# Linear-attention scan of a two-layer block: order of gates and low parts changed, layer 0's scan joined to its projection

## The chip, the core and the metric

The kernel runs on one core of a Trainium2 chip. The metric is device time in microseconds for one execution. All matrix products are done on TensorE as three products of split operands: each float32 matrix is held as a high part (rounded to the engine's fast fp32r form) and a low part (what the rounding left out), and high x high, high x low and low x high are summed.

## The reference, cut to what matters

Two blocks follow each other over 1024 tokens of width 1024. The change touches only the first, which has two layers. A layer normalises its input, projects it, and runs a linear-attention branch and a differential-attention branch beside each other:

```
h = rms_norm(x, g) * (1 + scale) + shift;  proj = h @ w_in
gq, gk, gv = silu(causal_depthwise_conv(concat(gq, gk, gv), conv_w))       # 8 tiles of 128 channels
log_a = log_sigmoid(glr @ w_gk + b_gk) / 16,  b = cumsum(log_a) in chunks of 64 tokens
k_dec = k * exp(b_end - b);  u = k_dec^T v;  state = exp(b_end) * state + u;  o = q state
o = rms_norm(o) * silu(z)
x = x + gate * (concat(o_gla, o_diff) @ w_out)
```

`shift`, `scale` and `gate` come from one vector: `mod = silu(c) @ w_ada + b_ada`. Those of the next layer are computed in the course of this one.

## The kernel before

The kernel is a row of stages. Within a stage each engine (SyncE for the DMAs, GpSimd, ScalarE, VectorE, TensorE) has a list of instructions in fixed order, and semaphores tie the lists together. Most stages are a block of their own, and a block ends with a barrier of all engines.

**Projection of the linear-attention branch** (`stage_gla_project`, L991, over the helper `stage_project`, L676). Jobs: four with 256 weight columns each, which give eight convolution tiles of two halves; one for `glr`; and the first half of the z weights, which is only loaded and split (`hold`), for use by the scan. For every tile TensorE makes two PSUM halves, ScalarE copies them to `u` (L866) and applies the first tap (L877), VectorE applies three more taps (L900), ScalarE applies SiLU (L883). In layer 0 VectorE also sums the modulation of layer 1: 16 parts of 512 KB are loaded into two buffers (`load`, L951; part k waits until part k-2 is summed) and accumulated with four instructions each (L961, L965). Two parts follow each convolution tile: parts 2n and 2n+1 behind tile n. At the very end VectorE makes the low part of the z weights (L788). ScalarE takes `glr` out of PSUM (L1010) behind the last SiLU.

**The scan** (`stage_gla`, L1072). It runs the recurrence over eight tiles of 128 tokens and, between its small products, 32 units of twelve 512-column matmuls (L1175) that project z and v. Each pair of units fills one PSUM bank (tiles 0 to 3 and 4 to 7 share four banks). Four units are done ahead (`LEAD`), then eleven steps n, each with three units, in TensorE's order: outputs of tile n-2 (L1240), transposes of tile n (L1193, L1195), a unit, decays of tile n-1 (L1211, L1213), gate product of tile n (L1202), a unit, states of tile n-1 (L1226), transposes of the result of tile n-3 (L1251), a unit. The decays write the bank from which `ktok` and `vtok` of the following tile are read, so they wait for both.

ScalarE's order in a step: squares of tile n-2 (L1324), `vtok` of tile n (L1300), root (L1332), decays (L1307), the gate's three functions (L1315 to L1319), `empty_y` (L1340). SiLU of the z units (`gates`, L1346) needs another function table than the rest and loads it, and the old one again: four tiles at the end of step 1 and four at the end of step 3. The high parts of the scan's four weight tiles (L1063) stand before the steps and at the ends of steps 2, 3 and 7. GpSimd makes the low parts (L1068) as soon as the high ones are there.

VectorE's order in a step: `ktok` (L1386), the normed result (L1427), `kdec` (L1394), the log gate (L1401), the state update (L1415), the copies of the summed gate (L1441), four accumulations of this layer's gate vector (L965), copies of v units (L1435). In layer 0 the last thing TensorE does is `columns` (L975): 32 products of one column that turn the sums for the next layer into columns, from which VectorE makes `shift` and `gain`.

**After the scan** the next block projects the differential branch (L824 again). In layer 1 the projection is preceded in its block by the output stage of layer 0, so its scan has always begun a new block.

Of the kernel before, what the change touches and what calls it, by code (L numbers as in the profile page):

```python
# [15 lines left out]
F32 = mybir.dt.float32  # L16
# [903 lines left out]
class Modulation:  # L920
# [52 lines left out]
    def columns(self, pe, bank, c0):  # L973
        for c in range(2 * KC):
# [16 lines left out]
def stage_gla_project(nc, m, jobs, feat, glrT, mod, b_gate, base, block, opening):  # L991
# [3 lines left out]
    nconv = 8  # L995

# [37 lines left out]
    def sp_job(sp, q, t):  # L1034
        if t == 0:
            mod.load_bias(sp, q, b_gate)
        for n in range(mod.early):
            if t == (0 if n < 2 else (n + 6) // 4):
# [6 lines left out]
                  sp_job=sp_job, begun=0 if opening else KC - 2, base=base, block=block, opening=opening)  # L1045


class ScanWeights:
# [7 lines left out]
    def __init__(self, nc, ctx, m, stage, jobs, slots):  # L1056
        self.nc, self.m, self.jobs, self.slots = nc, m, jobs, slots
        self.s_raw, self.s_hi, self.s_lo = semaphores(nc, ctx, m, stage, "wraw whi wlo")
        self.raw = ctx.enter_context(m.tensor(stage + "_wraw", [P, KC // 2 * 512], F32))
# [10 lines left out]


def stage_gla(nc, m, feat, glrT, zv, w_gk, b_gk, jobs, mod, slot):  # L1072
# [9 lines left out]
    with ExitStack() as ctx:  # L1082
        (s_w, s_turn, s_kv, s_gate, s_abs, s_act, s_la, s_suf, s_dec, s_kd, s_u, s_st, s_o, s_sq, s_r,
         s_y, s_yt, s_mix, s_dve, s_unit, s_slot, s_zev, s_vev, s_mraw0, s_mraw1, s_macc, s_spread, s_gated,
         s_own, s_wzero) = semaphores(
            nc, ctx, m, "gla", "w turn kv gate abs act la suf dec kd u st o sq r y yt mix dve unit slot zev vev mraw0 "
            "mraw1 macc spread gated own wzero")

        def sb(name, shape):
            return ctx.enter_context(m.tensor("gla_" + name, shape, F32))  # L1090

        wgk = sb("wgk", [RANKS + 1, GLA_QK])
        ktok, vtok = sb("ktok", [P, 2, GLA_QK]), sb("vtok", [P, 2, GLA_W])
        la, dec = sb("la", [P, 2, GLA_QK]), sb("dec", [P, 2, GLA_QK])
        gexp = sb("gexp", [P, GLA_QK])
        aend = sb("aend", [P, 2, 4])
        kdec = sb("kdec", [P, 2, GLA_QK])
        state = sb("state", [P, 4, pairs, GLA_DV])
        sq, ssq, r = sb("sq", [P, GLA_H, GLA_DV]), sb("ssq", [P, 2, GLA_H]), sb("r", [P, 2, GLA_H])
        y = sb("y", [P, 2, GLA_W])  # L1100
        weights = ScanWeights(nc, ctx, m, "gla", jobs, [1 - slot, 1 - slot, slot, slot])
        ps = m.ps
        block = ctx.enter_context(nc.Block())


        U, KG, TB = (4, 7), 5, 6
        STEPS = range(NT + 3)
        LEAD, UNITS, BANKS = 4, 4 * NT, 4
        n0 = mod.early
        late = len(mod.parts) - n0  # L1110

        def part_of(n):
            return n

        def o_of(h):
            return ps[:, U[h % 2], P * (h // 2):P * (h // 2) + P]

        def unit(u):


            job, w = u // 16, u % 16
            block4 = w // 4
            second = block4 in (1, 2)
            tile = w % 4 + 4 * (block4 // 2)
            return job, tile, second, block4 % 2 == 0

        def slot_of(job, second):
            return slot if job == second else 1 - slot

        @block.sync  # L1130
        def _(sp):
            load_tile(sp, weights.raw, weights.jobs[0], weights.s_raw)
            sp.wait_ge(s_wzero, 1)
            sp.dma_start(wgk[0:RANK, :], w_gk).then_inc(s_w, 16)
            sp.dma_start(wgk[RANK_LO:RANKS, :], w_gk).then_inc(s_w, 16)
            sp.dma_start(wgk[RANKS:RANKS + 1, :], b_gk).then_inc(s_w, 16)
            for k in range(2):
                mod.load(sp, (s_mraw0, s_mraw1), s_macc, n0 + k, n0)
            for k in range(2, late):
                if k in (part_of(3), part_of(5), part_of(7)):  # L1140
                    w = 1 + (part_of(3), part_of(5), part_of(7)).index(k)
                    sp.wait_ge(weights.s_lo, w)
                    load_tile(sp, weights.raw, weights.jobs[w], weights.s_raw)
                mod.load(sp, (s_mraw0, s_mraw1), s_macc, n0 + k, n0)
            m.clear_stale(sp)

        @block.gpsimd
        def _(pool):
            pool.memset(wgk[:, :], 0.0).then_inc(s_wzero, 1)
            weights.low(pool)  # L1150

        @block.tensor
        def _(pe):
            def project(u):
                job, tile, second, opens = unit(u)
                if u == 4:
                    pe.wait_ge(weights.s_lo, 1)
                if u == 16:
                    pe.wait_ge(weights.s_lo, 2)
                if u == 20:  # L1160
                    pe.wait_ge(weights.s_lo, 3)
                if opens and job == 0 and tile >= BANKS:
                    pe.wait_ge(s_zev, tile - BANKS + 1)
                if opens and job == 1 and tile < BANKS:
                    pe.wait_ge(s_zev, BANKS + tile + 1)
                if opens and job == 1 and tile >= BANKS:
                    pe.wait_ge(s_vev, tile - BANKS + 1)
                out, toks = ps[:, tile % BANKS, :], slice(P * tile, P * tile + P)
                hi, lo = (t[:, slot_of(job, second), :].rearrange("p (c n) -> p c n", c=KC // 2)
                          for t in (m.w_hi, m.w_lo))  # L1170
                for c in range(KC // 2):
                    lc = KC // 2 * second + c
                    a_hi, a_lo = m.hT_hi[:, lc, toks], m.hT_lo[:, lc, toks]
                    for k, (l, r) in enumerate(((a_hi, hi[:, c, :]), (a_hi, lo[:, c, :]), (a_lo, hi[:, c, :]))):
                        mm = nc.tensor.matmul(out, l, r, start=(opens and c == 0 and k == 0),  # L1175
                                              stop=(not opens and c == KC // 2 - 1 and k == 2))
                if not opens:
                    mm.then_inc(s_unit, 1)
                elif u in (11, 27):
                    mm.then_inc(s_slot, 1)  # L1180

            def turn(i):

                toks = slice(P * i, P * i + P)
                if i >= 1:
                    pe.wait_ge(s_kv, 2 * i)
                    pe.wait_ge(s_la, i)
# [3405 lines left out]
```

## Time and profile before

| | |
|---|---|
| median of 3 runs | 2449.79 us (2449.46 to 2450.44) |
| the profiled execution | 2450.71 us, its span 2449.0 us |
| TensorE busy | 2338.1 us, 95% of the span |
| VectorE, ScalarE, GpSimd busy | 1259.6 us, 1056.0 us, 632.8 us |
| TensorE clock granted, mean | 0.982 |
| layer 0: first product of the scan to first of the next stage | 156.65 to 297.79 us |
| layer 1: the same | 748.43 to 884.62 us |

Times inside the span are counted from its start. The busy time of TensorE counts a matmul at either clock alike, so the granted clock of a stretch has to be read beside it: 1.00 is 2.4 GHz, 0.50 is 1.2 GHz, and values between are mixtures of the two.

### The profile page before, as it was taken

The page shows a single profiled execution, that of the slowest core. Times are in us where ns is not written, and L with a number is a line of the kernel's source. Part 1 is how long each engine was busy: PE and PEld are TensorE (multiplying, and loading weights), DVE is VectorE, ACT ScalarE, POOL GpSimd, SP SyncE. Part 2 cuts the span into 40 slices and gives each one's busy share as a digit, 9 for nine tenths or more (in the row PEclk, how much of TensorE's full clock was granted, in tenths as well). Part 3 has the DMA queues.
Part 4 walks back from the last instruction along what each step waited for, and adds up shares of the span by engine and source line. Part 5 has one row for each costly group of instructions (what it writes and reads, how often), then busy time and mean ns, then how long its engine had stood idle before and what let it go on. Part 6 is the DMA issues. An engine that isn't in the chain of part 4 may idle for free. (4 is left out here: it accounts for less than half of the span.)

```text
span 2449.0 us, 33123 instructions
## 1 busy us (share of the span) xinstructions
PE 2338.1 (95%) x12824; PEld 1905.5 (78%) x12824; DVE 1259.6 (51%) x1768; ACT 1056.0 (43%) x2254; POOL 632.8 (26%) x419
## 2 busy tenths in 40 slices
PE   6998999889999999988999999998999999999999
PEld 4776787777887777777888887677888888888887
DVE  5854403785552520586553166561586777774121
ACT  4435313674543432376342546563653333334221
POOL 2201021133310122033232112112224444466130
PEclk8999999899999999999999999999999999999999
DMA  7432010103212211002211100003222222237231
GB/s 248 129 130 70 27 52 18 35 1 123 101 43 70 70 52 35 18 19 85 96 60 46 57 1 5 18 14 129 78 78 78 91 82 86 78 132 251 82 138 43
DMA packets 139073, 181.87 MB, mean 74 GB/s; under 512 B 8700, under 2 KB 102307, under 8 KB 138917
## 3 DMA queue, kind: packets, MB, share of 16 engines
q1 hardware_dynamic: 137877, 179.74, 21.4%
q8 instruction: 103, 1.69, 0.3%
q14 instruction: 53, 0.43, 0.1%
q10 hardware_dynamic: 1040, 0.00, 0.0%
HBM read 151.41 MB, written 28.31 MB: 73 GB/s over the span
## 5 line engine op out<-in xcount | busy, mean ns | idle before, releaser
L824 PE MATMUL ps<-w_hi,hT_hi 128*128 128x512 f32 (+1 forms) x384 | 142.8, 372 | 1.8 <-PEq L1082 1.8
L824 PE MATMUL ps<-hT_hi,w_hi 128*128 128x512 f32 x360 | 141.2, 392 | 2.8 <-PEq L274 2.8
L824 PE MATMUL ps<-w_hi,hT_lo 128*128 128x512 f32 (+1 forms) x384 | 142.8, 372 | 0.0
L824 PE MATMUL ps<-w_lo,hT_hi 128*128 128x512 f32 (+1 forms) x384 | 142.8, 372 | 0.0
L3978 POOL TENSOR_TENSOR w_lo<-ffn_sums,w_hi 128x512 fp32r<-128x512 f32 x76 | 96.7, 1294 | 171.9 <-ACT w_hi L4160 171.9
L824 PE MATMUL ps<-hT_lo,w_hi 128*128 128x512 f32 x360 | 140.6, 390 | 0.0
L824 PE MATMUL ps<-hT_hi,w_lo 128*128 128x512 f32 x328 | 128.3, 391 | 0.0
L1175 PE MATMUL ps<-w_hi,hT_hi 128*128 128x512 f32 x256 | 110.0, 430 | 12.9 <-ACT vd L1346 6.6
L4028 PE MATMUL ps<-ffn_t_hi,w_hi 128*128 128x512 f32 x304 | 118.4, 389 | 0.7 <-DVE ffn_u L4337 0.7
L4028 PE MATMUL ps<-ffn_t_hi,w_lo 128*128 128x512 f32 x304 | 118.3, 389 | 0.0
L4028 PE MATMUL ps<-ffn_t_lo,w_hi 128*128 128x512 f32 x304 | 118.3, 389 | 0.0
L2105 PE MATMUL ps<-w_hi,hT_hi 128*128 128x512 f32 x288 | 113.4, 394 | 4.3 <-PEq L4528 3.0
L2105 PE MATMUL ps<-w_hi,hT_lo 128*128 128x512 f32 x288 | 112.7, 391 | 0.0
L2105 PE MATMUL ps<-w_lo,hT_hi 128*128 128x512 f32 x288 | 112.5, 391 | 0.0
L4337 DVE TENSOR_TENSOR ffn_u<-ffn_u,ps 128x512 f32<-128x512 f32 x95 | 65.1, 685 | 80.4 <-PE ps L4028 77.4
L1175 PE MATMUL ps<-w_lo,hT_hi 128*128 128x512 f32 x256 | 103.9, 406 | 0.0
L1175 PE MATMUL ps<-w_hi,hT_lo 128*128 128x512 f32 x256 | 103.7, 405 | 0.0
L1828 ACT ACTIVATE big<-ps,att_nb 128x640 f32<-128x640 f32 (+7 forms) x128 | 94.2, 746 | 16.2 <-DVE att_nb L1815 15.6
L900 DVE SCALAR_TENSOR_TENSOR glap_cv<-glap_u,cols,glap_cv 128x1024 f32<-128x1024 f32 x48 | 74.6, 1555 | 46.6 <-ACT glap_cv L877 45.5
L1510 DVE TENSOR_REDUCE qk_ssq<-difp_sq 128x8 f32<-128x512 f32 x16 | 11.0, 686 | 168.6 <-ACT difp_sq L1498 168.6
L1815 DVE TENSOR_REDUCE att_nb<-ps 128x1 f32<-128x640 f32 (+7 forms) x88 | 86.5, 1022 | 18.7 <-PE ps L1805 18.5
L1068 POOL TENSOR_TENSOR w_lo<-gla_wraw,w_hi 128x2048 fp32r<-128x2048 f32 x8 | 37.1, 4636 | 212.3 <-ACT w_hi L1063 212.3
(564 smaller groups left out, 6534.5 us busy)
## 6 DMA issues: line engine op xcount, KB each, us to landing
ffn_raw<-in_ffn_w_up SPq DMA_DIRECT2D x40, 512.0 KB, 4.6
mix_gla<-in_w_ada SPq DMA_DIRECT2D x32, 512.0 KB, 3.4
ffn_raw<-in_ffn_w_down SPq DMA_DIRECT2D x30, 512.0 KB, 4.4
xres<-big SPq DMA_DIRECT2D x24, 512.0 KB, 2.6
hid<-ffn_f SPq DMA_DIRECT2D x22, 512.0 KB, 2.6
ffn_sums<-hid SPq DMA_DIRECT2D x44, 256.0 KB, 3.6
difp_raw<-in_w_in SPq DMA_DIRECT2D x10, 1024.0 KB, 5.0
open_ada<-in_w_ada SPq DMA_DIRECT2D x8, 1024.0 KB, 9.8
```

Of the source, the lines that this page charges most:

```text
L824: mm = nc.tensor.matmul(out, l, r, start=(job.part != 1 and c == 0 and k == 0), stop=(job.evac and c == job.chunks - 1 and k == len(pairs) ...
L900: ins = nc.vector.scalar_tensor_tensor(out=cv, in0=u[:, j:j + S], scalar=self.tap_col(n, j), in1=cv, op0=ALU.mult, op1=ALU.add)
L1068: pool.tensor_tensor(self.m.w_lo[:, self.slots[k], :], self.raw[:, :], self.m.w_hi[:, self.slots[k], :].bitcast(F32), ALU.subtract).then_i ...
L1175: mm = nc.tensor.matmul(out, l, r, start=(opens and c == 0 and k == 0), stop=(not opens and c == KC // 2 - 1 and k == 2))
L1510: nc.vector.tensor_reduce(ssq[:, i, 0:G], groups(q.sq[:, i % 2, :]), AX_X, ALU.add).then_inc(q.extra["sum"], 1)
L1815: self.nc.vector.tensor_reduce(self.nb[:, n % 4, mp, 0:nh], self.s_of(n, mp), AX_X, ALU.max, negate=True).then_inc(self.s_neg, 1)
L1828: ins = self.nc.scalar.activation(self.p_of(n, mp)[:, k, :], self.s_of(n, mp)[:, k, :], ACT.Exp, bias=self.nb[:, b, mp, k:k + 1], accum_ou ...
L2105: mm = nc.tensor.matmul(out, l, r, start=(first and c == 0 and n == 0), stop=(last and c == KC // 2 - 1 and n == 2))
L3978: pool.tensor_tensor(lo, op.source(n), hi.bitcast(F32), ALU.subtract).then_inc(s_lo, 1)
L4028: mm = nc.tensor.matmul(ps[:, bank(s, acc), :], l[:, c, :], r_[:, c, :], start=(first and c == 0 and i == 0), stop=(c == 3 and i == 2), sk ...
L4337: nc.vector.tensor_tensor(dst, left, ps[:, bank(s, k), :], ALU.add).then_inc(signal, 1)
```

## The change

- The scan's body is no longer a block of its own: it takes a context, a block and `q`, the projection's buffers and semaphores. In layer 0 it runs in the projection's block, without a barrier between. There it uses the projection's `raw` for its weights and the convolution buffers for `state`, `sq` and `y`, and waits on the projection's semaphores. In layer 1 it keeps its own block.
- In layer 0 the first unit does its eight products with high weights first, and waits for the low weights only then. Before the first unit TensorE waits for all 16 modulation parts, before every leading unit for its bank.
- The modulation parts follow the convolution tiles otherwise: parts 0 to 9 as before, 10 to 12 behind tile 5, 13 to 15 behind tile 6, none behind tile 7.
- `columns` is split in four and stands behind the four leading units; the gains follow on VectorE before step 0.
- The low parts of the scan's weights are made by VectorE, in both layers: before the steps and at the ends of steps 2, 4 and 8.
- ScalarE does `vtok` before the squares; the SiLUs come two at the end of step 0, two at the end of step 1, four at the end of step 3; the third high part moves from step 3 to step 4.

The core of the diff, leaving out the scan's re-indentation:

```diff
+    def part_tile(k):
+        return k // 2 if k < 10 else 5 + (k - 10) // 3
...
-            for k in (2 * n, 2 * n + 1):
-                if k < mod.early:
+            for k in range(mod.early):
+                if part_tile(k) == n:
                     mod.accumulate(dve, s_mraw(q), q.extra["macc"], k, 0)
...
+    def low_one(self, dve, k):
+        dve.wait_ge(self.s_hi, k + 1)
+        self.nc.vector.tensor_tensor(self.m.w_lo[:, self.slots[k], :], self.raw[:, :],
+                                     self.m.w_hi[:, self.slots[k], :].bitcast(F32), ALU.subtract).then_inc(self.s_lo, 1)
...
+    if q:
+        state = q.cv[:, 0, :].rearrange("p (n h d) -> p n h d", n=4, h=pairs)
+        sq = q.cv[:, 1, 0:GLA_W].rearrange("p (h d) -> p h d", h=GLA_H)
+        y = q.u[:, 0, 0:2 * GLA_W].rearrange("p (b n) -> p b n", b=2)
...
+    LOW_AT = (2, 4, NT)
...
+        if q:
+            sp.wait_ge(q.s_lo, q.made)
         load_tile(sp, weights.raw, weights.jobs[0], weights.s_raw)
...
+        if q:
+            sp.wait_ge(q.extra["macc"], mod.HALF * mod.early)
...
-            weights.low(pool)
...
+            if u == 0 and q:
+                order = [(c, k) for ks in ((0, 2), (1,)) for c in range(KC // 2) for k in ks]
+            for c, k in order:
+                lc = KC // 2 * second + c
+                if u == 0 and q and (c, k) == (0, 1):
+                    pe.wait_ge(q.s_lo, q.made)
...
+            if i == 0 and q:
+                for b in (*U, KG, TB):
+                    pe.wait_ge(q.free[b], 2)
+                pe.wait_ge(q.extra["silu"], 8)
...
+        if q:
+            pe.wait_ge(q.s_hi, q.made)
+            pe.wait_ge(q.free[U[0]], 2)
+            pe.wait_ge(q.extra["macc"], mod.HALF * mod.early)
         for u in range(LEAD):
+            if q:
+                pe.wait_ge(q.free[u], (q.units - u + NBANK - 1) // NBANK)
             project(u)
+            if mod.ahead:
+                mod.columns(pe, U[0], 0, range(u * 2 * KC // LEAD, (u + 1) * 2 * KC // LEAD)).then_inc(s_cols, 1)
...
-                elif n == NT + 2 and mod.ahead:
-                    pe.wait_ge(s_gated, 2)
-                    mod.columns(pe, KG, 0).then_inc(s_spread, 1)
...
         for n in STEPS:
-            if 0 <= n - 2 < NT:
-                squares(n - 2)
             if n < NT:
                 values(n)
             if 0 <= n - 2 < NT:
+                squares(n - 2)
                 root(n - 2)
...
-            if n == 1:
-                gates(range(4))
+            if n == 0:
+                gates((0, 1))
+            if n == 1:
+                gates((2, 3))
             if n == 2:
                 act.wait_ge(s_slot, 1)
                 weights.high(act, 1)
             if n == 3:
-                gates(range(4, 8))
-                weights.high(act, 2)
+                gates((4, 5, 6, 7))
+            if n == 4:
+                weights.high(act, 2)
...
+        weights.low_one(dve, 0)
+        if mod.ahead:
+            dve.wait_ge(s_cols, LEAD)
+            mod.gains(dve, Count(dve, s_own), m.layer + 1, U[0], 0)
...
+            if n in LOW_AT:
+                weights.low_one(dve, 1 + LOW_AT.index(n))
...
+                if not block:
+                    retire(m)
                 stage_gla_project(nc, m, glas[l], m.big, glrT, mod,
-                                  a["b_ada"][l, 2 * D:3 * D].rearrange("(c p) -> c p", c=1), base, block, opening)
+                                  a["b_ada"][l, 2 * D:3 * D].rearrange("(c p) -> c p", c=1), base, block, opening,
+                                  None if block else scan)
                 if block:
                     block.__exit__(None, None, None)
-                retire(m)
+                    retire(m)
+                    with ExitStack() as c3:
+                        scan(c3, c3.enter_context(nc.Block()), None)
```

## Rows read from the trace of the kernel before

**Rows 1.** The page's engine table: busy us, share of the span, instructions.

```profile
PE 2338.1 (95%) x12824; PEld 1905.5 (78%) x12824; DVE 1259.6 (51%) x1768; ACT 1056.0 (43%) x2254; POOL 632.8 (26%) x419
```

**Rows 2.** Waits of TensorE, 140 to 300 us: total us, times, longest.

```profile
PE ps L1175 <- PEq L682: 5.2, 1, 5.2
PE ps L1175 <- ACT vd L1346: 3.3, 1, 3.3
PE ps L1211 <- ACT gla_vtok L1300: 2.0, 1, 2.0
PE ps L1211 <- DVE gla_ktok L1386: 0.9, 1, 0.9
```

**Rows 3.** TensorE by stretches: window, length, busy (instructions), granted clock, DMA share, GB/s.

```profile
151.47:169.99 18.52, 13.34 (x49) 0.82 0.35 115
187.96:192.50 4.54, 4.54 (x13) 0.62 0.00 0
214.88:217.83 2.95, 2.95 (x14) 1.00 1.06 398
247.26:259.73 12.47, 12.47 (x90) 1.00 0.13 43
748.43:759.43 11.00, 11.00 (x48) 1.00 0.59 195
777.59:782.96 5.37, 5.37 (x13) 0.51 0.00 0
297.79:301.45 3.66, 3.66 (x9) 0.55 0.69 213
```

**Rows 4.** ScalarE's timeline, layer 0: start, duration, operation [idle before <- releaser].

```profile
151.15 1.05 ACT L1010 ACTIVATE glrT<-ps 48x512 f32<-48x512 f32 x2
...
180.57 0.60 ACT L1300 ACTIVATE gla_vtok<-ps 128x512 f32<-128x512 f32 x1 [5.06 <-PE ps L1195]
...
187.31 2.06 ACT L1346 ACTIVATE vd<-ps 128x512 f32<-128x512 f32 x4
189.39 1.28 ACT L1347 ACT_TABLE_LOAD   x1
...
224.51 1.91 ACT L1063 ACTIVATE w_hi<-gla_wraw 128x2048 fp32r<-128x2048 f32 x1
```

**Rows 5.** VectorE's accumulations and GpSimd's low part, layer 0, same columns.

```profile
194.50 2.04 DVE L965 SCALAR_TENSOR_TENSOR gate<-mix_gla,cact,gate 128x256 f32<-128x256 f32 x4
...
206.56 6.27 DVE L965 SCALAR_TENSOR_TENSOR gate<-mix_gla,cact,gate 128x256 f32<-128x256 f32 x4
...
206.68 4.83 POOL L1068 TENSOR_TENSOR w_lo<-gla_wraw,w_hi 128x2048 fp32r<-128x2048 f32 x1 [38.28 <-ACT w_hi L1063]
```

**Rows 6.** VectorE at the end of layer 0's projection, same columns.

```profile
146.22 3.93 DVE L900 SCALAR_TENSOR_TENSOR glap_cv<-glap_u,cols,glap_cv 128x1024 f32<-128x1024 f32 x3 [2.98 <-ACT glap_cv L877]
...
154.04 2.28 DVE L788 TENSOR_TENSOR w_lo<-glap_raw,w_hi 128x2048 fp32r<-128x2048 f32 x1
```

**Rows 7.** TensorE at the scan's end and the next stage's start, both layers.

```profile
292.49 0.63 PE L1251 MATMUL ps<-ident,gla_y 128*128 128x128 f32 x4
293.26 3.73 PE L975 MATMUL ps<-ones,mix_gla 128*128 128x1 f32 x32
297.79 0.47 PE L824 MATMUL ps<-w_hi,hT_hi 128*128 128x512 f32 x1 [0.80 <-PEq L1082]
...
882.96 0.63 PE L1251 MATMUL ps<-ident,gla_y 128*128 128x128 f32 x4
884.62 0.47 PE L824 MATMUL ps<-w_hi,hT_hi 128*128 128x512 f32 x1 [1.03 <-PEq L1082]
```

**Rows 8.** Loads of modulation parts 12 and 15: issue, then us to landing.

```profile
131.74 0.37 SPq L951 DMA_DIRECT2D mix_gla<-in_w_ada  x1
mix_gla<-in_w_ada SPq DMA_DIRECT2D x1, 512.0 KB, 4.4
...
mix_gla<-in_w_ada SPq DMA_DIRECT2D x1, 512.0 KB, 3.6
```

More of the change, by code:

```diff
@@ L971, in spread_gate, with columns @@
                                      start=True, stop=True)
-    def columns(self, pe, bank, c0):
-        for c in range(2 * KC):
+    def columns(self, pe, bank, c0, chunks):
+        for c in chunks:
             mm = self.nc.tensor.matmul(self.m.ps[:, bank, c0 + c:c0 + c + 1], self.acc[:, P * c:P * c + P],
@@ L988, in gains, with stage_gla_project @@
                                                 in1=cols[:, m.C_NORM:m.C_NORM + KC], op0=ALU.add, op1=ALU.mult))
-def stage_gla_project(nc, m, jobs, feat, glrT, mod, b_gate, base, block, opening):
+def stage_gla_project(nc, m, jobs, feat, glrT, mod, b_gate, base, block, opening, scan):
     conv = ConvTiles(nc, CONV_K, lambda n, j: m.col(m.C_CONV + 8 * j + n), None,
@@ L1044, in stage_gla_project, with __init__ @@
                   setup=lambda ctx, q: conv.setup(ctx, q, "glap"), dve_before=dve_before, dve_after=dve_after,
-                  sp_job=sp_job, begun=0 if opening else KC - 2, base=base, block=block, opening=opening)
+                  sp_job=sp_job, begun=0 if opening else KC - 2, base=base, block=block, opening=opening, tail=scan)
 class ScanWeights:
-    def __init__(self, nc, ctx, m, stage, jobs, slots):
+    def __init__(self, nc, ctx, m, stage, jobs, slots, raw=None):
         self.nc, self.m, self.jobs, self.slots = nc, m, jobs, slots
         self.s_raw, self.s_hi, self.s_lo = semaphores(nc, ctx, m, stage, "wraw whi wlo")
-        self.raw = ctx.enter_context(m.tensor(stage + "_wraw", [P, KC // 2 * 512], F32))
+        self.raw = raw if raw is not None else ctx.enter_context(m.tensor(stage + "_wraw", [P, KC // 2 * 512], F32))
     def high(self, act, k):
@@ L4473, in build_first, with scan @@
                 mod = Modulation(nc, m, mix_gla, a["w_ada"], l)
+                slot = (len(glas[l]) - 1 + base) % 2
+                weights = [gate_half(a["w_in"][l], 1), *halved("v", [wtile(a["w_in"][l], C_DV, DIFF_W)], DIFF_W), diffs[l][0]]
+                def scan(c, block, q):
+                    stage_gla(nc, m, c, block, q, m.big, glrT, v, a["w_gk"][l],
+                              a["b_gk"][l].rearrange("(c p) -> c p", c=1), weights, mod, slot)
+                if not block:
+                    retire(m)
                 stage_gla_project(nc, m, glas[l], m.big, glrT, mod,
-                                  a["b_ada"][l, 2 * D:3 * D].rearrange("(c p) -> c p", c=1), base, block, opening)
+                                  a["b_ada"][l, 2 * D:3 * D].rearrange("(c p) -> c p", c=1), base, block, opening,
+                                  None if block else scan)
                 if block:
                     block.__exit__(None, None, None)
-                retire(m)
-                base = (len(glas[l]) - 1 + base) % 2
-                weights = [gate_half(a["w_in"][l], 1), *halved("v", [wtile(a["w_in"][l], C_DV, DIFF_W)], DIFF_W), diffs[l][0]]
-                stage_gla(nc, m, m.big, glrT, v, a["w_gk"][l], a["b_gk"][l].rearrange("(c p) -> c p", c=1), weights, mod,
-                          base)
+                    retire(m)
+                    with ExitStack() as c3:
+                        scan(c3, c3.enter_context(nc.Block()), None)
+                base = slot
             with keep:
```

654 lines of the change are left out of this document (325 added, 329 removed).

## The prediction

> **What bounds the kernel now.** I read the page's engine table first: TensorE is busy for 95% of the span [rows 1], so only time in which it stands still, or runs at its lower clock, can come back. Then the waits of TensorE in the two scan stages, because they are what the diff touches. In layer 0 they are four [rows 2]: 5.2 us at the block boundary between projection and scan, and inside the scan 3.3 us for ScalarE's `vd` (L1346), 2.0 us for its `vtok` (L1300), 0.9 us for VectorE's `ktok` (L1386). The three inner waits come again in layer 1, with the same lengths to 0.1 us; its boundary wait is 1.2 us.
>
> Third, the granted clock of the stretches [rows 3]. A normal stretch of twelve 512-column matmuls between two small groups takes 2.95 us. After the `vd` wait it takes 4.54 us at a mean clock of 0.62 in layer 0 and 5.37 us at 0.51 in layer 1; after the `vtok` wait 4.54 us again, in both layers (229.64 and 820.11, rows like the first). The 0.9 us wait leaves no such trace. The first 48 products of the scan take 13.34 us in layer 0 (156.65 to 169.99, the remainder of the row's 18.52 after the wait) and 11.00 us in layer 1, after a wait of only 1.2 us: 2.34 us of clock. A step without a stall takes 12.47 us. So each long stall is paid twice, as idle time and then at 1.2 GHz in place of 2.4 GHz.
>
> **The three inner stalls, both layers.**
> *`vd`, step 1.* ScalarE now does four SiLU evictions at the end of step 1: table load 1.28, four copies 2.06, table load 1.28 [rows 4], begun at 186.0, while TensorE has waited for the first freed bank since 187.96 - 3.28 = 184.7. In the changed order two of them come in step 0, where ScalarE is done with the gate at 175.5 (the 5.06 us of idle before 180.57) [rows 4]. 175.5 + 1.28 + 1.03 (half of 2.06) + 1.28 gives 179.1, and the next thing it must do, `vtok` of tile 1, is not ready before 180.6 [rows 4]. The second pair runs from 186.0 to 189.6 and its banks are asked for a step later, with about 3 us to spare once the stall is gone. The stall goes: 3.28 + 1.60 of clock in layer 0, 3.28 + 2.43 in layer 1. The added pair of table loads lies in idle ScalarE time, at nothing; bare it would be 2.6 us a layer.
> *`ktok`, step 3.* At 206.56 VectorE's four accumulations take 6.27 us, where the same four take 2.04 elsewhere, because GpSimd's 4.83 us low part runs beside them [rows 5]; the `ktok` copy behind them came at 213.2, and TensorE had waited 0.9 for it, since 212.3. In the changed kernel VectorE accumulates until 208.6, makes the low part itself (2.28, the price of the same 128x2048 form on VectorE [rows 6]) until 210.9 and copies `ktok` (0.4) by 211.3. So 0.9 us go, with 1.0 to spare. If the low part took what GpSimd takes, 4.8, `ktok` would be 1.5 us late: those are the two ends, and the row of the same form decides for 2.28.
> *`vtok`, step 4.* ScalarE's four SiLUs end with the table load at 224.5; then come a 1.91 us weight copy and, until `vtok` (0.6) can begin at 227.4, 1.0 us of squares [rows 4]. The change puts both behind it: 224.5 + 0.6 = 225.1, while TensorE, which got it at 228.0 after 2.0 of waiting, asks at 226.0. 2.05 of idle and 1.60 of clock go in each layer. Next in line: the weight copy moves to the end of step 4, followed by VectorE's low part. Counted from that step's start, without stalls: last transposes done at 9.6, `big` copy 0.7, weight copy 1.9, low part 2.3: ready at 14.6, and the unit that needs it comes 5.5 into the next step of 12.47, at 18.0; `ktok` of that step stands behind the low part and is done at 15.0, asked for at about 16. In step 8 the last low part stands ahead of `vd` copies for which TensorE no longer waits; I charge nothing, at most 2.3 a layer.
> Sum: layer 0, 3.3 + 0.9 + 2.0 + 1.6 + 1.6 = 9.4; layer 1, with 2.4 for the first 1.6, 10.2 to 10.3. I take no part of it off; the low end, if one of the three waits stays in each layer, is 3.7 less per layer.
>
> **The column sums (layer 0 only).** 32 one-column matmuls of 3.73 us stand at the stage's very end, and the next stage starts 0.80 us after them [rows 7]. Layer 1 has no such sums: there the last transposes start at 882.96 and the next stage at 884.62, so 1.66 us later. In layer 0 they start at 292.49 and the next stage at 297.79, 5.30 later. Taking the sums away is worth 5.30 - 1.66 = 3.6. Besides, layer 0's next stage starts at a clock of 0.55: nine matmuls in 3.66 us [rows 3], where at full clock (48 in 11.00) it would be 16; 7 x 0.23 = 1.6 us more, which layer 1 does not pay. The same 32 products now stand between the leading units: +3.7 us. Bounds for them: nothing, if they fill waiting time, to 7.5 at half clock.
>
> **The join of layer 0.** The 5.2 us wait ends when VectorE, last of all, has made the low part of the z weights: convolution of tile 7 from 146.22 to 150.15, accumulation of two modulation parts until 154.1, low part 2.28 until 156.3, then the barrier [rows 6]. Without the barrier the first unit needs its bank back (after the last convolution: SiLU, about 1.0, and `glrT`, 0.6 [rows 4]), the high part (there) and all modulation parts; the low part comes in only after eight products. Were the convolution still done at 150.15, TensorE would go on at 151.8, almost without a gap.
> But parts 13 to 15 now stand ahead of that convolution. Part 12 is issued at 131.74 and lands 4.4 later, at 136.1 [rows 8]; accumulated until 138.1; convolution 6 (3.93) until 142.0; part 13 (2.02) until 144.1, part 14 until 146.1; part 15 may be issued only at 144.1, because its buffer is that of part 13, and lands 3.6 later at 147.7; accumulated until 149.7; convolution 7 until 153.7; SiLU and `glrT` 1.6: 155.3. If part 12 lands a microsecond earlier, 154.3. I take 155.0: 1.7 us gained of 5.2, ends 1.3 and 4.9. The gap stays at 3.5 us, longer than the 2.05 us after which the clock was seen at its lower level, so the 2.34 us of slow lead stay too. Behind the low part stand SP's load of the next weights, issued at about 156 (before, at the barrier's end, 156.6), the same copy on ScalarE (1.9), and VectorE's 2.28 in place of GpSimd's 4.8: all ready earlier than before, for a unit that comes later than before, at 155.0 + 11.0 + 2.3 + 3.7 = 172. The state memset and the gains (0.5) lie beside the lead, at nothing.
> The Trainium skill ("TensorE: Matmul & The Clock Gate", "Part 1: The HAM clock gate") says that the half-rate clock is the default and that activity releases it. By it, one-column products scattered in a lead that begins slow could keep the lead slow; the trace shows only that after 3.73 us of them in a block the clock is low [rows 3, 7], and that groups of small matmuls between units do not lower it (12.47 us steps at full clock). By the rule at its worst the lead costs 3.7 more for the columns and about 7 for three units; by the row, nothing.
>
> **Sum.** Layer 0: -9.4 - 3.6 - 1.6 + 3.7 - 1.7 = -12.6. Layer 1: -10.3. Together -22.9; I write -23. The stages behind begin with a TensorE-bound projection and a barrier, so all of it arrives at the end. The profiled execution took 2450.71 us (span 2449.0 and 1.7 around it): 2427.7 changed. The median of the three runs is 0.9 below the profiled one: 2426.8.
>
> **Rivals.**
> *A, the join gives everything.* Part 15 is not late, or is accumulated in time: TensorE goes on at 151.8, no slow clock: another 3.2 + 2.3, 2421.3. For it: the layer-1 boundary with 1.2 us shows a full clock. Against: the arithmetic of the two buffers above. 9%.
> *B, ScalarE or VectorE stays the bound in the scan.* The spare times above are 1.0, 0.9 and 1 us. If `vtok` or `ktok` is still late once per layer and the clock falls again (3.7 each): 2434; with the column products at half clock too, 2438. For it: `r` comes 0.6 later because squares now stand behind `vtok`, and all three low parts stand ahead of `ktok` copies. Against: each chain was reckoned from rows with its spare time. 17%. The Trainium skill ("ScalarE: Activation LUTs", "What ACT_TABLE_LOAD costs") gives a drain of about 1.38 us beside each load and advises to finish one table set before switching, which speaks against pairs. By that figure the first pair would end at an estimated 181.9 instead of 179.1 and TensorE, asking at the end of its next unit, some 3 us after the turn at about 180, still would not wait; no run here shows the drain, an activation starts right behind the load.
> *C, the clock of layer 0 stays down.* Starting slow, thinned by one-column products, TensorE could stay at 1.2 GHz through the lead and on into the scan. A unit costs about 2.4 us more at the low clock; from about ten units beyond the usual one on, the gain of 23 is eaten; low through the lead and the first three steps (12 units beyond it, 28.8, and 3.7 for the columns) it is 32.5 us: 2459. Against: from 161.5 on the clock rises in five us of products in a row. 4%.
> *D, the change hardly acts* (the stalls move to another engine at the same size, or clock and waits appear in later stages): within 5 us of before, 2449. 5%.
> My forecast holds 65%, with its own range 2423 to 2431.
>
> **How the numbers follow.** 0.2% is 4.9 us, about what a measurement of this kernel can tell from no change. Faster: forecast, A and B, 91%, less 1 for the tail of B: 0.90. Same 0.05, slower 0.05. The range goes from A's side, 2419, to B's worse end, 2438.
>
> **What would show it.** Waits of TensorE in both scans: L1346, L1300 and `ktok` gone, clock 1.00 from the first turn on; gap between projection and scan in layer 0 near 3.5 us, ended by ScalarE's `glrT`, with convolution 7 ending at about 153.7; layer 0's next stage at full clock; no GpSimd work in the scans. Wrong would be: a wait for `vtok` or `ktok` of over 0.5 us, a low clock after the first unit of step 0, or convolution 7 ending before 151.

## The result, and the profile after

The changed kernel took 2426.95 us in the median of four runs (2421.88 to 2428.38), the kernel before 2450.11 (four runs): the ratio is 0.990, 95% interval 0.988 to 0.992, so faster by 23.2 us. The forecast was 2426.8. The profiled execution took 2426.89 us, its span 2424.8. Layer by layer the forecast was less exact than the total, as will be seen.

The waits of TensorE in both scan stages come first, as [rows 2]: first from 140 to 300 us, then from 700 to 900.

```profile
PE ps L1191 <- ACT glrT L1013: 3.1, 1, 3.1
PE ps L824 <- PEq L682: 1.0, 1, 1.0
...
PE ps L1191 <- PEq L4521: 1.2, 1, 1.2
PE ps L824 <- PEq L4523: 1.0, 1, 1.0
```

The three inner waits are gone in both layers. Of the 5.2 us at the boundary of layer 0, 3.1 are left, now for ScalarE's `glrT`, not for a barrier. The stretches of TensorE that answer to [rows 3] (window, length, busy, granted clock, DMA share, GB/s):

```profile
150.03:169.13 19.10, 15.97 (x80) 0.91 0.34 112
183.80:186.74 2.94, 2.94 (x13) 1.00 0.00 0
227.93:240.40 12.47, 12.47 (x91) 1.00 0.40 127
732.41:743.40 10.99, 10.99 (x48) 1.00 0.58 195
758.00:760.95 2.95, 2.95 (x14) 1.00 0.00 0
283.33:286.99 3.66, 3.66 (x16) 1.00 0.69 223
```

The twelve products in which the `vd` wait was followed by a low clock now take 2.94 and 2.95 us in place of 4.54 and 5.37. The next stage of layer 0 starts with 16 products in 3.66 us, not nine. A step without a stall takes 12.47 us as before. Only the lead of layer 0 is still partly at the low clock.

ScalarE in layer 0, as [rows 4]: the first pair of SiLUs, `vtok` of tile 1 behind it, the four SiLUs of step 3 and `vtok` of tile 4.

```profile
152.44 1.05 ACT L1013 ACTIVATE glrT<-ps 48x512 f32<-48x512 f32 x2
...
176.01 1.09 ACT L1373 ACTIVATE vd<-ps 128x512 f32<-128x512 f32 x2
177.12 1.28 ACT L1374 ACT_TABLE_LOAD   x1
179.76 0.60 ACT L1327 ACTIVATE gla_vtok<-ps 128x512 f32<-128x512 f32 x1 [1.36 <-PE ps L1215]
...
214.19 2.06 ACT L1373 ACTIVATE vd<-ps 128x512 f32<-128x512 f32 x4
216.28 1.28 ACT L1374 ACT_TABLE_LOAD   x1
217.57 0.60 ACT L1327 ACTIVATE gla_vtok<-ps 128x512 f32<-128x512 f32 x1
```

The added table loads end 1.36 us before ScalarE is wanted again. `vtok` of tile 4 is done at 218.2; TensorE asks for it at 218.9, so 0.8 us are spare where the forecast had 0.9. VectorE, first at the end of the projection (as [rows 6]), then around the place of [rows 5]:

```profile
134.50 0.35 DVE L961 TENSOR_SCALAR mix_gla<-mix_gla,cact 128x256 f32<-128x256 f32 x1 [1.98 <-DMA mix_gla<-in_w_ada]
...
136.34 3.92 DVE L900 SCALAR_TENSOR_TENSOR glap_cv<-glap_u,cols,glap_cv 128x1024 f32<-128x1024 f32 x3
...
145.56 2.05 DVE L965 SCALAR_TENSOR_TENSOR mix_gla<-mix_gla,cact 128x256 f32<-128x256 f32 x4 [1.51 <-DMA mix_gla<-in_w_ada]
147.52 3.92 DVE L900 SCALAR_TENSOR_TENSOR glap_cv<-glap_u,cols,glap_cv 128x1024 f32<-128x1024 f32 x3
151.36 2.29 DVE L788 TENSOR_TENSOR w_lo<-glap_raw,w_hi 128x2048 fp32r<-128x2048 f32 x1
...
200.80 2.04 DVE L965 SCALAR_TENSOR_TENSOR gate<-mix_gla,cact,gate 128x256 f32<-128x256 f32 x4
202.76 2.29 DVE L1076 TENSOR_TENSOR w_lo<-glap_raw,w_hi 128x2048 fp32r<-128x2048 f32 x1
204.96 0.42 DVE L1417 COPY gla_ktok<-ps 128x256 f32<-128x256 f32 x1
```

VectorE stands still for part 12 (1.98 us) and for part 15 (1.51 us), and convolution 7 ends at 151.4, after the projection's last product at 150.0. In the scan the accumulations take 2.04 us again, and `ktok` is done at 205.4, 1.1 us before TensorE asks at 206.5.

The end of layer 0's scan, as [rows 7]: the next stage follows the last transposes by 1.66 us in place of 5.30.

```profile
281.67 0.63 PE L1273 MATMUL ps<-ident,glap_u 128*128 128x128 f32 x4
283.33 0.47 PE L824 MATMUL ps<-w_hi,hT_hi 128*128 128x512 f32 x1 [1.03 <-PEq L682]
```

### The profile page after: what moved, and what is told of

It reads as the page before. It is cut to its first block and busy times, and to the rows that moved or that the text cites. A ratio compares the mean times of both kernels' runs of the same rounds, so it can differ in the third digit from the quotient of the medians.

```text
span 2424.8 us, 33122 instructions
## 1 busy us (share of the span) xinstructions
PE 2329.8 (96%) x12824; PEld 1901.2 (78%) x12824; DVE 1266.4 (52%) x1776; ACT 1063.2 (44%) x2258; POOL 596.5 (25%) x411
## 5 line engine op out<-in xcount | busy, mean ns | idle before, releaser
L755 POOL TENSOR_TENSOR w_lo<-difp_raw,w_hi 128x2048 fp32r<-128x2048 f32 x8 | 36.8, 4604 | 391.3 <-ACT w_hi L724 391.3
```

What stands on the lines that cost most here:

```text
L755: pool.tensor_tensor(m.w_lo[:, b, 0:w], raw[:, 0:w], m.w_hi[:, b, 0:w].bitcast(F32), ALU.subtract).then_inc(s_lo, 1)
```

## The experiments

All were timed beside the kernel before on the same chip. In what follows "layer 0" and "layer 1" are the time from the projection's last product to the next stage's first, in one profiled execution: 146.3 and 137.4 us in the kernel before, 133.3 and 126.3 in the changed one. "Lead" is the time from the first leading unit to the first transposes.

**Pairs alone**, on the kernel before.

```diff
-                if n == 1:
-                    gates(range(4))
+                if n == 0:
+                    gates((0, 1))
+                if n == 1:
+                    gates((2, 3))
```

> The kernel before with one edit: the first four SiLU evictions in two pairs, at the ends of steps 0 and 1, in both layers. Theory (the vd wait is a wait for ScalarE's turn, each inner stall stands alone): the 3.3 us wait at L1346 goes in both layers, and the slow stretch behind it (4.54 for 2.95 in layer 0, 5.37 for 2.95 in layer 1): 5.0 + 5.8 = 10.8 us less, about 2439.3; the ktok wait (0.9) and the vtok wait (2.0) stay as they are. Rival (the two extra table loads push vtok): a new wait for vtok of tile 1 of 1 us or more in each layer, the gain at most half: 2444.

Measured: 2434.66 against 2450.64, ratio 0.9938 (0.9926 to 0.9951), 16.0 us less. The waits of layer 0:

```profile
PE ps L1175 <- PEq L682: 5.2, 1, 5.2
PE ps L1211 <- ACT gla_vtok L1300: 2.1, 1, 2.1
PE ps L1211 <- DVE gla_ktok L1388: 0.9, 1, 0.9
```

The `vd` wait alone is gone, as the theory had it, and no new one stands in its place; the rival falls. But the gain is half as large again as expected: 7.0 us in layer 0 and 7.3 in layer 1, where 5.0 and 5.8 were expected. The reason is in the stretch behind the `vtok` wait; the wait itself is as long as before, 2.1 us:

```profile
222.55:225.50 2.95, 2.95 (x13) 1.00 0.00 0
806.49:809.44 2.95, 2.95 (x13) 1.00 0.00 0
```

In both layers the clock did not fall behind it. In the kernel before it had, and cost 1.6 us each time. Most of what is left of the 16.0 us lies ahead of the scan, where the edit changes nothing: the projection ended at 149.8 us in place of 151.5.

**`vtok` first and the weight copy later**, on the kernel before.

```diff
-                if 0 <= n - 2 < NT:
-                    squares(n - 2)
                 if n < NT:
                     values(n)
                 if 0 <= n - 2 < NT:
+                    squares(n - 2)
                     root(n - 2)
...
                     gates(range(4, 8))
+                if n == 4:
                     weights.high(act, 2)
```

> The kernel before with vtok ahead of the squares and the third weight copy moved from step 3 to step 4, low parts still on GpSimd. Theory: the vtok wait of step 4 goes with its slow stretch, 2.2 + 1.6 in each layer, 7.6 us less: about 2442.5; the vd and ktok waits stay. Rival (the moved copy is late in turn, with GpSimd's 4.6 us behind it): a wait of TensorE at L1175 for w_lo in step 5, of 1 us or more; gain 3 us or less: 2447.

Measured: 2447.78 (eleven runs, 2443.36 to 2451.70), ratio 0.9986 (0.9978 to 0.9995): 2.9 us less, not 7.6. The `vtok` wait is gone from both layers and no wait for `w_lo` came, so the rival's mechanism fell. Layer 1 became 3.6 us shorter, close to the 3.8 expected, layer 0 only 2.4: there the clock now fell behind the `ktok` wait, whose length had not changed. The stretches behind the `vd` wait (as slow as before) and behind the 0.9 us `ktok` wait in layer 0, and behind the `ktok` wait in layer 1:

```profile
187.10:191.64 4.54, 4.54 (x12) 0.62 0.00 0
214.02:218.56 4.54, 4.54 (x13) 0.62 0.80 304
803.61:806.56 2.95, 2.95 (x13) 1.00 1.07 400
```

A 0.9 us wait was followed by the low clock once and by the full one once, in the same execution. The prediction's "leaves no such trace" was two observations, not a rule. A further 2.9 us came back far behind the edit: from the start of the second block's scan to the end of the span this execution took 1081.1 us, the kernel before 1078.2.

**Low parts on VectorE alone**, on the kernel before.

```diff
+    def low_one(self, dve, k):
...
             pool.memset(wgk[:, :], 0.0).then_inc(s_wzero, 1)
-            weights.low(pool)
...
             own.settle()
+            weights.low_one(dve, 0)
...
                         mod.accumulate(dve, (s_mraw0, s_mraw1), s_macc, n0 + k, n0)
+                if n in (2, 4, NT):
+                    weights.low_one(dve, 1 + (2, 4, NT).index(n))
```

> The kernel before with the scan's four low parts made by VectorE (first before the steps, then at the ends of steps 2, 4 and 8), nothing else. Theory (the ktok wait comes from the accumulations standing still under GpSimd's low part): the four accumulations of step 2 take 2.04 us instead of 6.27, the ktok wait of 0.9 goes in both layers, about 2 us less: 2448; vd and vtok waits stay. Rival (VectorE's order is the cause, the low part takes GpSimd's place): the ktok wait stays at 0.9 or grows to 1.5 or more: 2450 to 2453.

Measured: 2448.40 (twelve runs, 2443.22 to 2455.66), ratio 0.9992 (0.9982 to 1.0002): 2.2 us less in the median, which the interval does not tell from nothing. The trace decides on the wait: the one for `ktok` is gone in both layers, the others are as before. The gain in time can't be read from the layers, 3.1 us less in layer 0 and 0.5 more in layer 1, because the 2.1 us `vtok` wait was followed by the full clock in layer 0 and by a longer low stretch than before in layer 1 (0.56 over the 7.7 us from 815.43 on, where the kernel before has 0.78 over as many behind the same wait):

```profile
227.28:230.23 2.95, 2.95 (x13) 1.00 0.00 0
818.33:823.11 4.78, 4.78 (x14) 0.59 0.00 0
```

**Low parts back on GpSimd**, in the changed kernel.

```diff
         pool.memset(wgk[:, :], 0.0).then_inc(s_wzero, 1)
+        weights.low(pool)
...
-        weights.low_one(dve, 0)
...
-            if n in LOW_AT:
-                weights.low_one(dve, 1 + LOW_AT.index(n))
```

> The changed kernel with the scan's low parts back on GpSimd, nothing else. Theory: the ktok wait of step 3 comes back with about 1 us in both layers, since VectorE's accumulations again take about 6 us beside GpSimd, nothing else over 0.5 us; too short for the clock to fall: about 2 us more than the changed kernel, 2429. Rival (the waits of the scan are coupled, and without the others this one grows, because the stretch ahead of it is shorter): a wait of 2 us or more with a slow stretch behind it, 3.7 us or more per layer: 2434 or more.

Measured: 2430.83, ratio 0.9917 (0.9904 to 0.9929), 3.9 us over the changed kernel as timed first; the intervals of the two ratios overlap, so the trace has to decide. The wait for `ktok` is back, 0.9 and 1.0 us, and it did not grow. VectorE's row is that of before:

```profile
202.44 6.27 DVE L965 SCALAR_TENSOR_TENSOR gate<-mix_gla,cact,gate 128x256 f32<-128x256 f32 x4
208.62 0.42 DVE L1418 COPY gla_ktok<-ps 128x256 f32<-128x256 f32 x1
```

From the first transposes to the next stage it takes 115.4 and 115.6 us, against 114.2 and 114.1: 2.7 us more, with the full clock behind both waits. The direction was right, and GpSimd's share in the stall is shown from both sides.

**Layer 0 not joined**, else as changed.

```diff
-                                  None if block else scan)
+                                  None)
                 if block:
                     block.__exit__(None, None, None)
                     retire(m)
-                    with ExitStack() as c3:
-                        scan(c3, c3.enter_context(nc.Block()), None)
+                with ExitStack() as c3:
+                    scan(c3, c3.enter_context(nc.Block()), None)
```

> The changed kernel with layer 0's scan in a block of its own again, all else as changed (16 parts by tile 6, columns in the lead). Theory (the join is worth little, because convolution 7 now waits for part 15, and the barrier only adds the low part and itself): the gap between projection and scan is 4.0 us instead of 3.1, and the lead somewhat slower: 1 to 2 us more than the changed kernel, 2428 to 2429. Rival (the join carries the layer-0 gain): 5 us more, 2432.

Measured: 2427.18, ratio 0.9910 (0.9894 to 0.9927). The gap is 4.2 us, the lead 16.9, layer 0 takes 135.3 us: 2.0 more than in the first profiled execution of the changed kernel, 0.5 more than in a later one (134.7, below). The join makes the gap 0.9 to 1.1 us shorter; in the medians it is worth 0.2 us, less than the runs of either kernel spread. The rival's 5 us are out.

**The parts in the old order**, else as changed.

```diff
-        return k // 2 if k < 10 else 5 + (k - 10) // 3
+        return k // 2
```

> The changed kernel with the modulation parts two behind each convolution tile, as before the change. Convolution 7 then ends near 148.7 (151.4 in the changed kernel), but TensorE waits for the sum of all parts, until about 152.7. Theory (both orders end at the same point, because the parts gate the columns in one and the convolution in the other): the gap stays within 0.6 us of 3.1, now ended by VectorE's accumulation, and the time within 1 us of the changed kernel. Rival (the new order of the parts is what shortens the gap): gap of 5 us, 2 us or more slower.

Measured: 2424.99, ratio 0.9898 (0.9883 to 0.9913), 2 us below the changed kernel rather than within 1 us of it. Convolution 7 ended at 147.3, 1.3 us before the projection's last product (1.4 us behind it in the changed kernel). Layer 0 takes 133.0 us, the gap is 2.9, and as expected it is VectorE's sum that ends it:

```profile
PE ps L1191 <- DVE mix_gla L965: 2.9, 1, 2.9
```

So both orders of the parts end at nearly the same point, and nothing shows that the new order brought a gain.

**The column sums back at the end**, else as changed.

```diff
...
+            elif n == NT + 2 and mod.ahead:
+                pe.wait_ge(s_gated, 2)
+                mod.columns(pe, KG, 0, range(2 * KC)).then_inc(s_spread, 1)
...
-            if mod.ahead:
-                mod.columns(pe, U[0], 0, range(u * 2 * KC // LEAD, (u + 1) * 2 * KC // LEAD)).then_inc(s_cols, 1)
...
+            elif n == NT + 2 and mod.ahead:
+                dve.wait_ge(s_spread, 3)
+                mod.gains(dve, Count(dve, s_own), m.layer + 1, KG, 0)
...
-        if mod.ahead:
-            dve.wait_ge(s_cols, LEAD)
-            mod.gains(dve, Count(dve, s_own), m.layer + 1, U[0], 0)
```

> The changed kernel with the column sums back at the end of layer 0's scan. Theory: the lead is 3.2 us shorter, the end 3.6 us longer, and the next stage begins at the low clock (nine products where 16 fit, 1.6 us): 2.0 us more than the changed kernel, 2429. Rival (the products are cost wherever they stand, and the clock at the end is chance): within 0.5 us of the changed kernel, and the next stage's first twelve products at full clock.

Measured: 2428.89, ratio 0.9914 (0.9900 to 0.9929), 1.9 us over the changed kernel, where 2.0 were expected. The lead is 12.3 in place of 16.0, the way from the first transposes to the next stage 117.9 in place of 114.2, and the next stage begins low:

```profile
283.69:287.35 3.66, 3.66 (x9) 0.50 0.66 203
```

That the low clock there is chance is refuted by the count: in all five profiled executions that have the block of column products at the end of layer 0, the next stage began at 0.50 to 0.60; in the nine without it, and in all fourteen of layer 1, at 1.00.

**The last two parts behind convolution 7 and the z low part.**

```diff
-        return k // 2 if k < 10 else 5 + (k - 10) // 3
+        return k // 2
...
-            for k in range(mod.early):
+            for k in range(mod.early - 2):
                 if part_tile(k) == n:
...
-            pe.wait_ge(q.extra["macc"], mod.HALF * mod.early)
...
-            if mod.ahead:
-                mod.columns(pe, U[0], 0, range(u * 2 * KC // LEAD, (u + 1) * 2 * KC // LEAD)).then_inc(s_cols, 1)
+            if mod.ahead and u >= 1:
+                if q and u == 1:
+                    pe.wait_ge(q.extra["macc"], mod.HALF * mod.early)
+                mod.columns(pe, U[0], 0, range((0, 4, 10)[u - 1], (4, 10, 16)[u - 1])).then_inc(s_cols, 1)
...
+        if q:
+            for k in range(mod.early - 2, mod.early):
+                mod.accumulate(dve, (q.extra["mraw0"], q.extra["mraw1"]), q.extra["macc"], k, 0)
         weights.low_one(dve, 0)
...
-            dve.wait_ge(s_cols, LEAD)
+            dve.wait_ge(s_cols, LEAD - 1)
```

> The changed kernel with the last two modulation parts summed behind convolution 7 and behind the low part of the z weights; TensorE waits for the sums only after the second leading unit, where the first columns now stand (columns behind leading units 2, 3 and 4). Theory (part 15's load, held back by its buffer, delays convolution 7 and with it the bank of the first unit): convolution 7 ends near 148.7, TensorE goes on 0.3 to 0.6 us after the projection instead of 3.1, and the lead runs at full clock: 3 + 1.4 = 4 us less than the changed kernel, 2422.7. Rival (something else holds the first unit, or another wait takes its place behind it): gap over 2 us, or a wait for the sums of 2 us or more; time as changed.

Measured: 2421.75, ratio 0.9886 (0.9871 to 0.9901). TensorE's wait in layer 0, its stretch from the projection's end to the first transposes, and VectorE around convolution 7:

```profile
PE ps L1191 <- ACT glrT L1013: 0.4, 1, 0.4
```

```profile
149.73:164.73 15.00, 14.61 (x80) 1.00 0.43 143
```

```profile
144.48 3.93 DVE L900 SCALAR_TENSOR_TENSOR glap_cv<-glap_u,cols,glap_cv 128x1024 f32<-128x1024 f32 x3 [2.97 <-ACT glap_cv L877]
148.32 2.29 DVE L788 TENSOR_TENSOR w_lo<-glap_raw,w_hi 128x2048 fp32r<-128x2048 f32 x1
...
150.92 0.35 DVE L961 TENSOR_SCALAR mix_gla<-mix_gla,cact 128x256 f32<-128x256 f32 x1
151.30 3.67 DVE L965 SCALAR_TENSOR_TENSOR mix_gla<-mix_gla,cact 128x256 f32<-128x256 f32 x7
```

Convolution 7 ends at 148.4, the sums at 155.0, before the end of the second leading unit, behind which they are asked for. The gap is 0.4 us and the lead runs at full clock: 14.6 us, of which 11.0 are the units (as in layer 1) and 3.6 the columns. Layer 0 takes 129.2 us. The step of the prediction that a held-back load delays the bank of the first unit is shown by taking it away, together with TensorE's early wait for the sums; the old order above, which took away only the first, left the gap at 2.9 us.

**The changed kernel and this one once more**, side by side.

> The changed kernel itself, beside the next one on the same chip: 2427, with a spread of some us between executions from the clock behind short waits.

> The kernel with the last two modulation parts behind convolution 7 once more, beside the changed kernel. Theory: its layer 0 from the end of the projection to the next stage is 4.1 us shorter than in the changed kernel in any execution (0.4 us of waiting and a full clock in the lead), so its median is 3 to 5 us below the changed kernel's. Rival (the difference between the two first measurements was chance of the clock in later stages): the medians within 1 us.

Measured: 2426.96 (2425.27 to 2427.50) and 2421.13 (2419.79 to 2422.26); against before 0.9908 (0.9893 to 0.9923) and 0.9885 (0.9870 to 0.9900). The runs don't overlap: 5.8 us between the medians, a little over the 3 to 5 expected. Layer 0 took 134.7 and 129.2 us, 5.5 us apart where 4.1 "in any execution" had been expected: the lead of the changed kernel took 17.2 us this time, not 16.0. The kernel with the parts behind is thus the faster one in both comparisons.

**Seven and fourteen products more** in the changed kernel's lead, to move everything behind them.

```diff
             project(u)
+            if u == 0 and q:
+                for _ in range(7):
+                    nc.tensor.matmul(ps[:, U[0], :], m.hT_hi[:, 0, 0:P], m.w_hi[:, slot_of(0, False), 0:512], start=True,
+                                     stop=True)
```

> The changed kernel with seven more 512-column products behind layer 0's first leading unit, into a bank that is overwritten afterwards: 1.6 us more of TensorE at 0.229 each, nothing else. Theory (whether the clock falls behind a short wait depends on the moment at which the wait comes, not on the wait alone): all waits behind stay as long as in the changed kernel, but at least one of the short waits of the later stages (1.0 us before the projections, 1.35 us before the second block's scan) changes its side, full clock where it was low or the reverse, and the span differs by other than 1.6 us, by up to 3 either way. Rival (the low stretches belong to the waits and to what was done before them): the same stretches are low with the same losses, and the span is 1.6 us longer, to 0.3.

> The same with fourteen products, 3.2 us. Theory: again another set of low stretches behind short waits, with the waits themselves unchanged. Rival: the same set as in the changed kernel, and 3.2 us more.

Measured: 2428.83 (0.9917, 0.9900 to 0.9933) and 2429.49 (0.9919, 0.9904 to 0.9933): 1.9 and 2.5 us over the changed kernel beside them, where 1.6 and 3.2 us of products had been added. Layer 0 took 135.5 and 138.4 us. The place to look at is the start of the second block's scan. TensorE's wait there is 1.35 us in the kernel before, in both executions of the changed one, and 1.4 with seven and fourteen products more. The first 3.66 us behind it, in the kernel before, in the changed kernel, and in its second profiled execution:

```profile
1370.77:1374.43 3.66, 3.66 (x16) 1.00 0.72 206
```

```profile
1343.62:1347.28 3.66, 3.66 (x9) 0.54 0.69 208
```

```profile
1343.66:1347.32 3.66, 3.57 (x16) 1.00 0.66 194
```

Seven more products, and fourteen, both left this stretch at full clock. But so did the second execution of the unaltered kernel, with the same instructions, at nearly the same time of the span and with the same wait. That speaks against the rival (the low stretches belong to the waits and to what was done before them), more plainly than the delays do; the delays themselves show no more than that execution does, and what decides in a single case stays open. Whether the two executions ran on the same chip is not known. But on one chip, too, this stretch was seen at both levels: at 1.00 in the kernels with layer 0 not joined and with the column sums at the end, at 0.53 and 0.54 in those with the parts in the old order and with the parts behind. The Trainium skill ("TensorE: Matmul & The Clock Gate", "Part 1: The HAM clock gate") says that the chip's watch over TensorE's activity runs freely and does not begin anew with a kernel. These runs agree with it (0.54 and 1.00 behind the same 1.35 us wait), but do not show it to be the reason.

## Why the prediction was right, step by step

| step | forecast us | measured us |
|---|---|---|
| inner stalls, layer 0 | -9.4 | -10.0 (first transposes to next stage 127.8 to 114.2, less 3.6 for the end) |
| inner stalls, layer 1 | -10.3 | -11.0 (125.18 to 114.14) |
| columns away from the end | -3.6 | -3.6 (5.30 to 1.66) |
| next stage's clock | -1.6 | -1.6 (9 to 16 products) |
| columns in the lead | +3.7 | +3.6 (14.6 less 11.0, from the kernel with the parts behind) |
| gap at the join | -1.7 | -2.0 (5.18 to 3.14) |
| low clock in the lead | 0 | -1.0 (2.34 to 1.36: 16.0 less 14.6) |
| all else | 0 | -1.4 ahead of the scan, about +2.9 behind it |

*The three stalls* went as reckoned, each for the named reason: the trials with one edit each took away its own wait and left the others. Their spare times came out within 0.2 us of the forecast (0.8 and 1.1 for 0.9 and 1.0). The low part on VectorE costs 2.29 us, forecast 2.28. The sum was 0.6 and 0.7 us too small. It took a stall for no more than its wait and the clock behind it, and a stall costs some tenths more: with the low parts back on GpSimd, waits of 0.93 and 0.99 us made the way to the next stage 1.2 and 1.5 us longer, at full clock throughout.

*The columns.* Both terms held. In four groups between units they cost as much as in a block, and they did not keep the lead at the low clock: rival C did not come.

*The join.* The mechanism held to the instruction: part 12 is waited for, part 15's load is held back by its buffer, and the bank of the first unit comes behind the SiLU of convolution 7. From the projection's end, convolution 7 ended 1.4 us later, where 155.0 had meant about 1.9. By the clock of the span it ended at 151.4 and not at 153.7, near the 151 named as a sign of being wrong; 1.4 us of that are only the earlier end of the projection. The forecast took the gap for 3.5 us and it was 3.1 in one execution and 3.35 in another. The term with the wrong size is the clock of the lead: 2.34 us in the forecast, 1.36 measured, in a second execution 2.6 (17.2 less 14.6).

*"All of it arrives at the end"* is the sentence that failed. The profiled stages became 25.7 us shorter (13.0 and 11.1, and 1.6 of the next stage), the opening stages took 1.4 us less, and the span fell by 24.2. Behind the two scans 2.9 us were given back: the second block's scan began 27.1 us earlier, the last product of the kernel 24.2. 1.8 of it lie between the start of that scan and the wait of 3.0 us some 307 us later, 1.6 of them in the slow first stretch shown above, and 1.3 in the 110 us behind that wait, which ran at a somewhat lower mean clock, first before, then changed:

```profile
1677.51:1786.70 109.19, 107.14 (x496) 0.99 0.33 121
1652.14:1762.59 110.45, 108.37 (x496) 0.97 0.32 120
```

Nothing ties either to the change. The instructions there are the same, and over all fourteen profiled executions the time from the start of the second block's scan to the end of the span went from 1078.2 to 1082.5 us: 1078.2 in the kernel before, in that with pairs alone and in that with low parts on VectorE, 1081.1 in the kernel before with `vtok` first, 1081.2 and 1079.4 in the two of the changed kernel. The end of the projection, where nothing before it was meant to get faster, spread likewise, from 148.6 to 151.5 us. So the -1.4 and the +2.9 of the table are differences of one execution each.

The prediction read the low clock as a property of a wait's length ("longer than the 2.05 us after which the clock was seen at its lower level"). In the two scan stages, at the start of the stages behind them and at the start of the second block's scan, over all fourteen profiled executions, waits of 2.9 us and more were followed by a low stretch in all 18 cases, waits of 2.05 us in three of six, of 1.35 us in five of 14, of 0.9 to 1.0 us in the scans in one of eight, of 1.0 us ahead of the next stage and of 1.2 us ahead of layer 1's scan in none of 23 and 14, of 0.4 us in neither of two. Elsewhere not even the first of these held: in the opening stages a wait of 3.0 us was followed by the low clock in the first profiled execution of the changed kernel (0.50, from 24.00 us on) and by the full one in the second (1.00, from 25.53 on). So the total was right partly by luck: a gain sized 2.8 us too small met a loss of about the same size that had not been seen.

Rival A is refuted for this kernel, and the kernel with the parts behind shows what it had priced at 5.5 us: 4.1 in the first profiled execution, 5.5 in the second. Rival B did not come. Of D, clock lost in later stages came with 2.9 us, but it left the gain nearly whole.

## What to carry to other kernels

A stall of the bound engine is best read as two entries, the wait and the stretch behind it, and only the wait may be counted in full: here the clock behind waits of 0.9 to 2.05 us came out differently from one execution to the next, so a forecast should carry it as spread, and a verdict on a change of a few microseconds should rest on the waits and stage lengths in the trace, not on the difference of medians. Before work is moved ahead of something that TensorE needs, look for the buffer that its load waits for: here that wait cost more than the barrier that was taken away, and moving two of 16 parts behind the critical convolution was worth 4.1 to 5.5 us, the join 0.5 to 2.0.

## What the runs showed of the hardware that was not expected

- The same instructions with the same 1.35 us wait ran at full clock in one execution and at the low clock in another, 1.6 us apart; the clock behind a 0.9 us wait was 0.62 in one case and 1.00 in the seven others.
- Four accumulations on VectorE take 2.04 us alone and 6.27 us beside a GpSimd subtraction of 128x2048 elements; the same subtraction takes 2.29 us on VectorE and 4.83 us on GpSimd.
- 32 one-column products cost 3.6 to 3.7 us, in a block or spread. Behind a block of them and a wait of 0.80 us the next stage began at 0.50 to 0.60 of full clock in five executions of five; behind a wait of 1.03 us without the block it began at 1.00 in 23 of 23.
